# Wide dense matmuls in a hybrid encoder block's pair stage, halves joined by VectorE, and a spacer ahead of the squared activations

## What is computed

```
xn   = RMSNorm(h)
cols = xn @ w_in  -> [q | k | v | RWKV r, k, v + low-rank parts | two merge gates]
o_attn = windowed attention ;  o_rwkv = forward scan + backward scan of 32 heads of 64
mix  = (sigmoid(g_attn) * o_attn + sigmoid(g_rwkv) * o_rwkv) @ w_out
h    = h + RMSNorm(mix)
h    = h + RMSNorm(relu(RMSNorm(h) @ w_ffn_up)^2 @ w_ffn_down)
```

## Time and profile before

| | us |
|---|---|
| median of 3 runs (lowest, highest) | 2063.53 (2062.06, 2068.5) |
| the profiled execution | 2065.07 |
| its span, first to last instruction | 2063.3 |
| TensorE busy in the span | 1993.1 (97%) |
| VectorE / ScalarE / GpSimd busy | 1317.3 / 927.3 / 371.0 |
| one pass of the pair loop | 53.3 |
| one chunk of the FFN (8 units up, 8 down; 8 chunks) | 90.9 |

### The profile page before, as it was taken

The page is one execution under the profiler, slowest core; times in us unless marked ns, Lnnn a source line. Parts: engine busy times, 40 slices in busy tenths (PEclk is TensorE's granted clock), DMA queues, the critical chain, the costliest instruction groups (busy, mean ns, idle before and its releaser), DMA issues.

```text
span 2063.3 us, 39449 instructions
## 1 busy us (share of the span) xinstructions
PE 1993.1 (97%) x14555; PEld 1841.9 (89%) x14555; DVE 1317.3 (64%) x2226; ACT 927.3 (45%) x1669; POOL 371.0 (18%) x438
## 2 busy tenths in 40 slices
PE   6999999899999999999999999999999999999997
PEld 6999999899999999999999878899898989989896
DVE  3666546677777777777777864655555555555554
ACT  4555433344444454545445543543443434334343
POOL 0000000333343333344444440100000000000001
PEclk9999999899999999999999999999999999999999
DMA  7555666433223333233331326356566565656553
GB/s 209 136 142 140 182 163 170 109 89 82 77 78 87 88 88 87 77 79 87 88 88 47 123 86 226 103 187 184 187 184 188 184 182 192 183 183 183 184 182 122
DMA packets 415375, 281.28 MB, mean 136 GB/s; under 512 B 14074, under 2 KB 372700, under 8 KB 414556
## 3 DMA queue, kind: packets, MB, share of 16 engines
q1 hardware_dynamic: 414908, 277.43, 46.5%
q10 hardware_dynamic: 416, 3.15, 0.4%
HBM read 278.46 MB, written 2.10 MB: 136 GB/s over the span
## 4 chain that ended last, share of the span: by engine, by line
PE 90%; DVE 3%; issue 2%; ACT 2%; POOL 1%; DMA 0%; SPq 0%; ACTq 0%; DVEq 0%; POOLq 0%
PE bank L1512 16%; PE bank L1513 15%; PE bank L1514 15%; PE bank L1532 6%; PE bank L1531 6%; PE bank L1530 6%; PE bank L1753 2%; PE bank L1797 2%; PE bank L1815 2%; PE bank L1820 2%; PE bank L1658 1%; PE bank L1882 1%; PE bank L1660 1%; PE bank L1861 1%; PE bank L1659 1%
## 5 line engine op out<-in xcount | busy, mean ns | idle before, releaser
L1512 PE MATMUL bank<-xT,whi 128*128 128x256 f32 x2784 | 823.6, 296 | 12.1 <-DVE wlo L848 8.0
L1513 PE MATMUL bank<-xT,whi 128*128 128x256 f32 x2784 | 789.1, 283 | 0.0
L1514 PE MATMUL bank<-xT,wlo 128*128 128x256 f32 x2784 | 788.4, 283 | 0.0
L1512 PEld LDWEIGHTS bank<-xT,whi 128*128 128x128 f32 x2784 | 535.1, 192 | 15.1 <-issue 9.1
L1513 PEld LDWEIGHTS bank<-xT,whi 128*128 128x128 f32 x2784 | 535.6, 192 | 1.9
L1514 PEld LDWEIGHTS bank<-xT,wlo 128*128 128x128 f32 x2784 | 534.1, 192 | 0.0
L848 DVE TENSOR_TENSOR wlo<-raw,whi 128x1024 fp32r<-128x1024 f32 (+1 forms) x164 | 247.0, 1521 | 58.7 <-ACT whi L440 54.1
L1353 DVE TENSOR_TENSOR wlo<-raw,whi 128x1024 fp32r<-128x1024 f32 x126 | 154.4, 1225 | 200.7 <-ACT whi L810 200.7
L810 ACT ACTIVATE whi<-raw 128x1024 fp32r<-128x1024 f32 x126 | 132.8, 1054 | 216.9 <-PE bank L1532 216.9
L1531 PE MATMUL bank<-wlo,ft 128*128 128x512 f32 x512 | 202.2, 395 | 0.0
L1532 PE MATMUL bank<-whi,ft 128*128 128x512 f32 x512 | 202.2, 395 | 0.0
(11 more groups left out here) (224 smaller groups left out, 3072.4 us busy)
## 6 DMA issues: line engine op xcount, KB each, us to landing
raw<-in_w_in SPq DMA_DIRECT2D x106, 1024.0 KB, 5.9
raw<-in_w_ffn_up SPq DMA_DIRECT2D x64, 1024.0 KB, 6.4
raw<-in_w_ffn_down SPq DMA_DIRECT2D x64, 1024.0 KB, 5.0
raw<-in_w_out SPq DMA_DIRECT2D x16, 1024.0 KB, 5.5
raw<-in_w_in SPq DMA_DIRECT2D x4, 768.0 KB, 4.6
xtok<-in_x SPq DMA_DIRECT2D x2, 1024.0 KB, 5.9
upg<-in_g_up SPq DMA_DIRECT2D x16, 128.0 KB, 3.4
hres<-in_x ACTq DMA_DIRECT2D x1, 2048.0 KB, 12.3
```

The lines of the kernel that those rows point to most:

```text
L1512: M(bank[:, 0:T], h, xT[:, k, 0, :], start=k == 0, stop=False)
L1513: M(bank[:, 0:T], h, xT[:, k, 1, :], start=False, stop=False)
L1514: x = M(bank[:, 0:T], l, xT[:, k, 0, :], start=False, stop=k == KT - 1)
```

## The change

1. **Pair units.** TensorE's `dense` no longer calls `unit_b`. For each k-step it gives two matmuls: `whi` with 512 columns moving (hi and lo parts of the activations side by side, which fills the whole bank), and `wlo` with 256 columns, added to the first half. Columns per k-step stay 768, weight loads fall from three to two.
2. **Joining.** ScalarE copies the first half to `raw4` as before, but raises the new `d_cp`. VectorE's new `dense(j, i)` waits for it, adds the bank's second half to the row in place, and raises `d_evac`. This is one more VectorE instruction for each of the 64 pair units, at six places in its order.
3. **A spacer.** A tile `ahead_of_ft` of 72 floats, 288 bytes, which nobody uses, is put ahead of `ft`. From `xT` to `ft` are then 83,968 bytes, which is 164 x 512. `fa`, `fs`, `junk` and `fin` move by 288 bytes too.

```diff
+        sb("ahead_of_ft", [P, 72], stack=ffn)
         ft = sb("ft", [P, 8, 2, T], f32r, stack=ffn)
@@ ScalarE
-                A.activation(raw4[:, slot, 1:T + 1], PB[u % 2][:, 0:T], ACT.Copy).then_inc(d_evac.sem, 1)
+                A.activation(raw4[:, slot, 1:T + 1], PB[u % 2][:, 0:T], ACT.Copy).then_inc(s["d_cp"].sem, 1)
@@ VectorE
+            def dense(j, i):
+                if isinstance(i, int) and i >= PAIRS:
+                    return
+                u = U_RW + j
+                dve.wait_ge(s["d_cp"].sem, s["d_cp"].at(i, j + 1))
+                row = raw4[:, (1, 0, 2, 3)[j], 1:T + 1]
+                V.tensor_tensor(row, row, PB[u % 2][:, T:2 * T], ALU.add).then_inc(d_evac.sem, 1)
...
+                        if l == 3 and d == 0:
+                            dense(2, d1)
...
+                dense(3, d1)
                 if nx:
                     nx.differences()
...
                             nx.inverse(0)
+                        dense(0, d2)
+                        if nx:
                             nx.modified()
...
                 cut_pair(0, d2, 1)
+                dense(1, d2)
                 cut_pair(1, d2, 0)
...
             for j in range(4):
+                dense(j, 0)
                 cut_pair(j, 0)
...
                     g0.bonus()
+                    dense(0, 1)
                     cut_pair(0, 1)
+            dense(1, 1)
             cut_pair(1, 1)
@@ TensorE
-                unit_b(U_RW + j, 4 * n + U_RW + j, k0, k1, s["x_free"] if last else None)
+                bank = PB[u_static % 2]
+                hi, lo = whi[:, u_static % 2, :], wlo[:, u_static % 2, :]
+                for k in range(k0, k1):
+                    M(bank[:, :], hi[:, P * k:P * k + P], xT[:, k, :, :], start=k == 0, stop=False)
+                    x = M(bank[:, 0:T], lo[:, P * k:P * k + P], xT[:, k, 0, :], start=False, stop=k == KT - 1)
```

More of the change, by code:

```diff
@@ L257, in block_kernel @@
             ex=4, esink=4, den=4, rden=4, prn=4, p_tp=4, p_T=4, pv=4, o_ev=4,
-            ga_m=4, lo_nb=1, lo_df=1, lo_sh=1, lo_act=1, lo_fin=1, drv=1, zr=1,
+            ga_m=4, lo_nb=1, lo_df=1, lo_sh=1, lo_act=1, lo_fin=1, drv=1, zr=1, d_cp=4,
             up_ld=1, sh_nb=1, sh_df=1, shifted=1, gate_t=1, sqd=1, ss=1, ssm=1, rs=1, rrep=1, rbc=1, nkk=1, gg=2,
@@ L1502, in _, with unit_b @@
             M = nc.tensor.matmul
-            def unit_b(u_static, u, k0=0, k1=KT, half_read=None):
+            def unit_b(u_static, u, k0=0, k1=KT):
                 if k0 == 0:
@@ L1514, in unit_b @@
                     x = M(bank[:, 0:T], l, xT[:, k, 0, :], start=False, stop=k == KT - 1)
-                    if half_read is not None and k == KT // 2 - 1:
-                        x.then_inc(half_read.sem, 1)
                 if k1 == KT:
@@ L1670, in dense @@
                     return
+                u_static, u = U_RW + j, 4 * n + U_RW + j
                 if k0 == 0:
-                    pe.wait_ge(d_evac.sem, d_evac.n(4 * n + U_RW + j - 1))
-                last = isinstance(n, int) and n == PAIRS - 1 and j == 3
-                unit_b(U_RW + j, 4 * n + U_RW + j, k0, k1, s["x_free"] if last else None)
+                    pe.wait_ge(d_evac.sem, d_evac.n(u - 1))
+                    pe.wait_ge(w_lo.sem, w_lo.n(u + 1))
+                bank = PB[u_static % 2]
[3 more added lines that the diff above has]
+                    x = M(bank[:, 0:T], lo[:, P * k:P * k + P], xT[:, k, 0, :], start=False, stop=k == KT - 1)
+                    if isinstance(n, int) and n == PAIRS - 1 and j == 3 and k == KT // 2 - 1:
+                        x.then_inc(s["x_free"].sem, 1)
+                if k1 == KT:
+                    x.then_inc(w_used.sem, 1)
             inc = lambda x, name: x.then_inc(s[name].sem, 1)
```

## The result

The changed kernel takes 2044.01 us (median of 4 runs, 2042.92 to 2045.11) where the kernel before takes 2063.61 (2062.06 to 2068.5). The ratio is 0.9895, 95% interval 0.9882 to 0.9909: 19 to 24 us less, where the forecast was 2048.0 with a range of 2042 to 2060. The profiled execution took 2043.11 us; its span is 22.0 us shorter than that of before.

The account below looks back on a forecast made before the run. The prediction took TensorE's pace from matmul to matmul as the bound. Pair units -5.9, VectorE's sums +0.35 (together -5.5) and the spacer -10.0 made -15.5 us: 2048.0 us, range 2042 to 2060.

Parts of the forecast that it names:

- What bounds the kernel: Whole kernel: time goes by how fast TensorE, busy 97% of the span, passes from one matmul to the next.
- Part 1, 6.7 ns for each matmul less: Pair units: two matmuls for three save 6.7 ns a k-step, -5.9 us in sum.
- the 54 k-steps: Pair loop: of 64 k-steps a pass, 54 gain; over 14 passes at 6.7 ns, 5.07 us.
- the near end of the 0.43 to 0.85 forecast: Four units of pair 0: 64 unbroken k-steps at 6.7 to 13.3 ns gain 0.43 to 0.85 us; 0.64 taken.
- The far end, 13.3 ns: Pair units: largest saving considered for each matmul less, as in unbroken rows; 6.7 ns was taken instead.
- Part 2, the sums in the passes: Pair loop: VectorE's four sums of 0.35 us a pass, 1.4 us, all hidden in idle time; cost 0.
- the last rival: Pair loop: VectorE becomes the bound, 2.43 us a pass, 34 us in all, 2082 us; chance 0.08.
- Part 2, ahead of the loop: Ahead of the loop: VectorE's added sums cost +0.35 us in all.
- +0.35, once: Ahead of the loop: sum of unit 0 of pair 1 delays the cut for which TensorE waits, by 0.35 us.
- Part 3, the spacer, -10.0 us: FFN down: if the standing block's start sets the pace, 1,536 matmuls gain 6.5 ns each, -10.0 us.
- The first rival: FFN down: the spacer does nothing, its pace having another cause; only -5.5 remains, 2058.0 us; chance 0.17.
- the quiet pace: Passes: 13.3 ns for each matmul less there too, a further 5.0 us, 2043.0 us; chance 0.09.

Follow-up runs that it names:

- e9: Changed kernel with FFN up also in the two-matmul form, each unit's 16 matmuls of 512 columns first, then the 16 of 256; 2034.74 us.
- e16: Changed kernel with whi, wlo and ft 32 bytes off a multiple of 64, and FFN up with 512 and 256 columns by turns; 2036.74 us.
- e11: Changed kernel with each of VectorE's sums made twice, the first time into a tile that nothing reads; 2048.66 us.
- e6: Kernel before with one idle VectorE instruction ahead of the loop, at the place of the sum of unit 1 of pair 1; 2059.67 us.
- e5: Changed kernel with the sum of unit 1 of pair 1 moved behind the weight cut, ahead of the loop; 2051.17 us.
- e1: Kernel before with only the 288 unused bytes ahead of ft; 2058.29 us.
- e2: Changed kernel without the 288 unused bytes ahead of ft; 2053.72 us.
- e3: Kernel before with 32 unused bytes ahead of ft; 2058.52 us.
- e12: Changed kernel with whi and wlo 32 bytes off a multiple of 64, all other tiles unmoved modulo 64; 2040.26 us.
- e18: Changed kernel with 352 unused bytes ahead of ft for 288; 2054.48 us.
- e15: Changed kernel with xT alone 32 bytes off a multiple of 64; 2029.17 us.
- e8: Changed kernel with FFN up also in the two-matmul form, 512 and 256 columns by turns; 2037.7 us.
- e10: Changed kernel with two-matmul FFN up, 512s grouped ahead of 256s there, in the pair loop's fillers and in the units ahead of it; 2033.89 us.

## Why the prediction was right or wrong

- **What bounds the kernel**: right. TensorE is still 97% busy and every gain came from its distances from start to start, or from the wait and the clock ahead of the loop.
- **Part 1, 6.7 ns for each matmul less**: right in the size. 13 passes gained 5.41 us, 0.416 each (0.64 the first, 0.40 each of the others), for 0.362 forecast. That is the 54 k-steps at 7.7 ns, or 62 at 6.7. Which of the two, the runs don't say for certain: the median filler of two, three and four k-steps in the 13 passes takes 0.753, 1.127 and 1.479 us for 0.769, 1.148 and 1.513, which is 8.0, 7.0 and 8.5 ns a k-step and speaks for the first. The four units of pair 0 take 22.61 us for 23.04: 6.7 ns for each of the 64, the near end of the 0.43 to 0.85 forecast; but they begin 0.4 us later in the profiled execution after, and end where they ended. The far end, 13.3 ns, was not seen anywhere in the changed kernel. Only what e9 and e16 changed, the 512 columns in a row of their like or another distance of `xT`, brought a k-step of 768 columns down to 347 ns from 353.
- **Part 2, the sums in the passes**: right, with a slip that changes nothing: the last rival's price of 2.43 us a pass is 2.45 by its own terms. The sum ahead of the differences has 0.94 us before it (forecast about 1.1), released by ScalarE's copy; the next right-hand side still idles 1.59 us; TensorE shows no wait for the squares. e11 puts a number on the cover that is left: of 1.4 us more a pass, about 1.1 were hidden.
- **Part 2, ahead of the loop**: the step that failed. "+0.35, once" looked only at the sum of unit 0, and part 1 gave the first two units of pair 1 a 0. The trace of before had a second wait of 2.12 us there, for DT of GpSimd, and a clock at half speed behind it; neither was read. The sum of unit 1 turns the order in which GpSimd's DT and VectorE's cut begin, and the stretch gave -4.9 us for a forecast of -0.65. By e6, about 4.1 of it are the wait and the clock; 0.36 are the wide units of the first pass (45.43 us to the first landmark for the 45.79 of e6), and 0.45 lie ahead of the wait for the cut weight and have no experiment. e5 takes the sum away from that place and loses 6 to 7 us, e6 adds only an idle instruction and gains 5.5.
- **Part 3, the spacer, -10.0 us**: right in the size and in what it acts on (-10.0 in e1, in e2 undone, and after). Wrong in the cause as told: not the start of the standing block but its distance from the block that moves. The forecast called the new distance between `xT` and `ft` "an exact multiple" of 512; that held the right answer only because `whi` lies a multiple of 256 from `xT`, which is luck. e3 gains as much at another place, and e12 and e18 lose with `ft` on a multiple of 64.
- **The first rival, a place that does nothing**: ruled out. The same 128x512 product takes 226.8 or 233.3 ns by 64 bytes (after and e18). The page "SBUF — State Buffer" (Operand start alignment) of the Trainium skill calls its rule on starts one of legality, not speed, and says that its runs timed nothing. So it neither foretold this nor denied it.
- **The norms' 1.6 us**: not in any case, and not owed to the change.
- **The range**: it began at 2042 with the quiet pace alone. No case let the part ahead of the loop gain. What the measured kernel has beyond the forecast comes for the greater part from there; the passes added 0.7 us, and the norms' 1.6 in those executions that had them.

## What to carry to other kernels

Where TensorE runs in long rows, measure its distance from start to start and try a few unused bytes, in steps of 32, between the tile that stands and the tile that moves: it gave 10 us here, and 15 more with `xT` moved as well (e15). Where VectorE and GpSimd both have long instructions ready at about the same time, put the one that TensorE waits for first, and read every wait around an inserted instruction together with the granted clock behind it, since a wait of 2 us cost 4 to 7 here (e6, e5).

## What the runs showed of the hardware that was not expected

- A 128x512 matmul takes 226.8 or 233.3 ns, and a 128x256 one 116.7 or 120.0, by the distance modulo 256 bytes of the two tiles it reads, in opposite senses for the two forms (table; 0, 32, 64 and 224 were tried for the first, 0 and 32 for the second).
- With weights standing, 512 and 256 columns take 353.2 ns together by turns in a long row (e8) and 347.7 when the 512s stand in a row of their like, at 226.9 each (e9). In rows of one to four k-steps the order makes no difference (e10).
- A GpSimd product of 128x512 takes 1.17 us when it begins ahead of VectorE's cut and 3.10 when it begins 0.2 us behind; the cut takes 3.18 or 2.29.
- After a wait of 2.1 us, the second of 1.7 to 2.1 us within 6 us, TensorE ran at the lower clock for 7 to 14 us while busy, with the same program up to there (before, e1). After the first of them alone it fell for 3 us in some executions and not in others (e10, e9).
